# A decoder layer on one core: norm factors from replicated sums, router in column groups, reordered GLA opening, early modulation products

## The reference, cut to what matters

```python
mod = silu(c) @ ada_w + ada_b                  # six groups of 1024: sh1, sc1, gt1, sh2, sc2, gt2
h = rmsnorm(x, norm_mix_w) * (1 + sc1) + sh1
# h @ w_in is split; three branches: gated DeltaNet (o_a), GLA (o_b), Conformer convolution (o_c)
o_a = o / sqrt(mean(o*o) + eps) * dn_norm_w * silu(dn_z)
log_a = log_sigmoid(glr @ gla_gate_w + gla_gate_b) / 16
o_b = gla_recurrence(gq * 64**-0.5, gk, gv, log_a, S0)   # then its own gated RMSNorm
x = x + gt1 * (merged @ w_out)
u = rmsnorm(x, norm_ffn_w) * (1 + sc2) + sh2
s = sigmoid(u @ router_w)                      # 64 experts; top 8 of them, then the experts
x = x + gt2 * moe(u)
```

## Time and profile before

| | |
|---|---|
| median of 3 runs | 2899.44 us |
| profiled execution's own time | 2898.27 us |
| its span, first to last instruction | 2896.5 us |
| TensorE busy | 2755.3 us, 95% |
| VectorE, ScalarE, GpSimd busy | 37%, 20%, 28% |
| mean granted TensorE clock | 0.971 of full speed |

### The profile page before, as it was taken

How to read it: one execution, slowest core, us unless ns; L and a number is a source line. 1 busy time by engine, 2 the same in 40 slices (tenths; PEclk the granted TensorE clock), 3 DMA queues, 4 the chain that set the end, 5 groups by cost and what they waited for, 6 DMA issues and landing times. The chain is left out here.

```text
span 2896.5 us, 31387 instructions
## 1 busy us (share of the span) xinstructions
PE 2755.3 (95%) x10366; PEld 1626.5 (56%) x10367; DVE 1058.4 (37%) x1635; ACT 572.8 (20%) x1074; POOL 813.1 (28%) x992
## 2 busy tenths in 40 slices
PE   7997999997999899999999898999999999999996
PEld 4564888864666556666666566444444444444443
DVE  3333233334657677832111273322222222222224
ACT  3213333324434200011000230111111111111112
POOL 1000222101334000000000012555655555565553
PEclk8998999998999999999999898999999999999997
DMA  6520000021010111212112120688777788888874
GB/s 239 226 96 25 16 16 23 15 67 33 23 44 23 46 28 34 72 33 80 48 26 102 46 104 0 233 283 270 242 250 208 257 300 280 282 265 264 294 241 145
DMA packets 162802, 382.19 MB, mean 132 GB/s; under 512 B 24595, under 2 KB 111711, under 8 KB 134793
## 3 DMA queue, kind: packets, MB, share of 16 engines
q1 hardware_dynamic: 130449, 311.52, 30.2%
q0 software_dynamic: 32256, 69.33, 10.4%
HBM read 339.65 MB, written 72.94 MB: 142 GB/s over the span
## 5 line engine op out<-in xcount | busy, mean ns | idle before, releaser
L2568 PE MATMUL ps<-big 128*128 x1536 | 675.5, 593 | 3.2 <-SPq L2495 1.8
L2568 PEld LDWEIGHTS ps<-big 128*128 128x128 f32 x1536 | 284.3, 190 | 325.7 <-issue 325.7
L2520 POOL DMA_INDIRECT big<-u_rows,big x384 | 393.7, 1025 | 169.9 <-issue 85.4
L1756 PE MATMUL ps<-big 128*128 128x352 f32 x1152 | 346.8, 461 | 5.7 <-SPq L1692 5.7
L2578 PE MATMUL ps<-big 128*128 x768 | 345.8, 593 | 3.4 <-ACT big L2632 3.4
L1756 PEld LDWEIGHTS ps<-big 128*128 128x128 f32 x1152 | 219.7, 191 | 129.1 <-SPq L1692 6.1
L2673 DVE SCALAR_TENSOR_TENSOR big<-big,ps 128x256 f32<-128x256 f32 x96 | 64.0, 667 | 570.9 <-ACT big L2622 570.7
L2578 PEld LDWEIGHTS ps<-big 128*128 128x128 f32 x768 | 145.4, 190 | 188.4 <-issue 188.4
L846 PE MATMUL ps<-big 128*128 128x352 f32 x576 | 206.0, 464 | 2.1 <-DMA big<-in_w_in 2.0
L1301 PE MATMUL ps<-big 128*128 128x352 f32 x576 | 187.1, 473 | 12.8 <-DVE big L1521 7.8
L2536 POOL DMA_INDIRECT y_rows<-big x96 | 155.9, 1624 | 126.6 <-issue 61.2
(11 more groups left out here) (557 smaller groups left out, 3120.7 us busy)
## 6 DMA issues: line engine op xcount, KB each, us to landing
big<-in_exp_w_gate SPq DMA_DIRECT2D x64, 1024.0 KB
big<-in_exp_w_up SPq DMA_DIRECT2D x64, 1024.0 KB
big<-in_exp_w_down SPq DMA_DIRECT2D x64, 1024.0 KB
big<-in_ada_w SPq DMA_DIRECT2D x24, 1024.0 KB, 7.5
big<-in_w_in SPq DMA_DIRECT2D x48, 512.0 KB, 4.1
big<-in_w_in SPq DMA_DIRECT2D x6, 1024.0 KB, 5.3
big<-in_w_branch SPq DMA_DIRECT2D x24, 256.0 KB, 4.5
big<-u_rows,big POOLq DMA_INDIRECT x384, 5.9
```

The source lines that it names most:

```text
L1756: ins = pe.matmul(ps[:, c, 0:CW], ring_g[:, q % 2, j, :], k.hT[:, j, c * CW:(c + 1) * CW], start=(j == 0), stop=(j == KT - 1))
L2520: g.indirect_dma_start(out=x_rows[:, u, x * 256:(x + 1) * 256], out_offset=None, in_=u_quarters, in_offset=bass.IndirectOffsetOnAxis(idx_i ...
L2568: ins = pe.matmul(ps[:, 2 + u, :].rearrange("p (g f) -> p g f", f=FF), xT[:, u, j, :], gate_up[:, j], start=(j == 0), stop=(j == KT - 1))
```

## The change

Four places are edited.

1. `setup`: TensorE runs the first three modulation products ahead of its wait for the inverted norm factors, so ahead of their spread.
2. `gla_rule`: ScalarE takes the DeltaNet norm's root right after draining z 0, ahead of the units of gates 1. VectorE makes `keys(0, 0)` right after the reciprocal and `keys(0, 1)` after half of the spread. The four multiplications by `z` go from VectorE to GpSimd, behind its `queries` of chunk 2.
3. `project_out`: root and reciprocal are taken on all 128 partitions of the sum, so the turning, the small reciprocals and the spreading matmuls go. A root of a constant stands at ScalarE's start of the block.
4. `project_out`: the router's product runs in four quarters of 264 columns, whose results go to partitions 0 to 63 and 64 to 127 in turn; ScalarE copies two quarters of the logits out, VectorE the other two.

```diff
             # setup, TensorE
+            pe.wait_ge(c_copied, 1)
+            for x in range(3):
+                pe.wait_ge(ada_loaded[x], 16)
+                ada_product(k, pe, 6, slots[x], x).then_inc(ada_used, 1)
             pe.wait_ge(inverted, 1)
-            pe.wait_ge(c_copied, 1)
...
-            for x in range(KT):
+            for x in range(3, KT):
             # gla_rule, ScalarE
-            drain(ends[order["gates", 1, NCH - 1]])
+            drain(ends[order["z", 0, NCH - 1]])
             act.wait_ge(by_dve, drains("sum"))
             act.activation(fac[0:8, :], fac[0:8, :], ACT.Sqrt).then_inc(rooted, 1)
+            drain(ends[order["gates", 1, NCH - 1]])
             decays(0, 0)
             # gla_rule, GpSimd, after the queries of chunk i
+                if i == 2:
+                    g.wait_ge(by_act, drains("z", 3))
+                    for h in range(H):
+                        g.tensor_tensor(z[:, h, :], z[:, h, :], src[:, h, :], ALU.mult).then_inc(oa_done, 1)
             # gla_rule, VectorE
-                            v.wait_ge(by_dve, drains("spread", H - 1))
-                            v.wait_ge(by_act, drains("z", 3))
-                            for h in range(H):
-                                ins = v.tensor_tensor(z[:, h, :], z[:, h, :], src[:, h, :], ALU.mult)
-                            ins.then_inc(oa_done, 1)
-                            v.wait_ge(oa_done, 1)
+                            v.wait_ge(oa_done, H)
...
             v.reciprocal(fac[0:8, :], fac[0:8, :]).then_inc(inverted, 1)
+            keys(0, 0)
+            drain(ends[order["spread", 1, NCH - 1]])
+            keys(0, 1)
             drain(first_steps)
-            for p in range(2):
-                keys(0, p)
             # project_out, TensorE (the turn L2017 and the spread L2023 go)
+                for q in range(4):
+                    ins = pe.matmul(ps[E_N * (q % 2):E_N * (q % 2) + E_N, 3 + q // 2, 0:LW], rw[:, j, :], k.hT[:, j, q * LW:(q + 1) * LW],
+                                    start=(j == 0), stop=(j == KT - 1))
             # project_out, ScalarE
+            act.wait_ge(eps_ready, 1)
+            act.activation(warm[:, :], eps[:, :], ACT.Sqrt)
...
-            act.wait_ge(eps_ready, 1)
             act.wait_ge(summed, 1)
+            act.activation(root[:, 0:2 * CW].rearrange("p (c w) -> p c w", c=2), ps[:, 6:8, 0:CW], ACT.Sqrt, scale=1.0 / D, bias=eps[:, :])\
                .then_inc(rooted, 1)
+            act.activation(root[:, 2 * CW:T], ps[:, 0, 0:CW], ACT.Sqrt, scale=1.0 / D, bias=eps[:, :]).then_inc(rooted, 1)
...
+            for q in (0, 2):
+                act.activation(k.logits_T[:, q * LW:(q + 1) * LW], ps[0:E_N, 3 + q // 2, 0:LW], ACT.Copy).then_inc(stopped, 1)
             # project_out, VectorE
+            for r, cols in enumerate((slice(0, 2 * CW), slice(2 * CW, T))):
+                v.wait_ge(rooted, r + 1)
+                v.reciprocal(root[:, cols], root[:, cols]).then_inc(inverted, 1)
+            v.wait_ge(inverted, 2)
...
-                v.tensor_tensor(k.hT[:, j, 0:SEQ], k.xT[:, j, 0:SEQ], wide, ALU.mult).then_inc(normed, 1)
+                v.tensor_tensor(k.hT[:, j, 0:SEQ], k.xT[:, j, 0:SEQ], root[:, 0:SEQ], ALU.mult).then_inc(normed, 1)
...
+            v.wait_ge(logits, 1)
+            for q in (1, 3):
+                v.tensor_copy(k.logits_T[:, q * LW:(q + 1) * LW], ps[E_N:2 * E_N, 3 + q // 2, 0:LW]).then_inc(copied, 1)
```

More of the change, by code:

```diff
@@ L1958, in project_out @@
     sq, acc, root = w.take(2, T), w.take(T), w.take(T)
-    rw, rstd, eps = w.take(KT, E_N), w.take(NT), w.take(1)
+    rw, eps, warm = w.take(KT, E_N), w.take(1), w.take(1)
+    LW = T // 4
     filled, drained, added = k.sem("po_filled"), k.sem("po_drained"), k.sem("po_samples_added")
     router_loaded, shared_loaded, eps_ready = k.sem("po_router_loaded"), k.sem("po_shared_loaded"), k.sem("po_eps_ready")
-    squared, gathered, summed, rooted, turned, inverted, spread, normed, sampled, modulated, logits, dstep, stopped = (
-        k.sem("po_" + x) for x in ("squared", "squares_added", "summed", "rooted", "turned", "inverted", "spread", "normed", "sampled",
-                                   "modulated", "logits", "dve_step", "logits_copied"))
+    squared, gathered, summed, rooted, inverted, normed, sampled, modulated, logits, dstep, stopped, copied = (
+        k.sem("po_" + x) for x in ("squared", "squares_added", "summed", "rooted", "inverted", "normed", "sampled",
+                                   "modulated", "logits", "dve_step", "logits_copied", "logits_copied_by_vector"))
     zeroed, zeros_stored = k.sem("po_zeroed"), k.sem("po_zeros_stored")
@@ L2013, in _ @@
             ins.then_inc(summed, 1)
[L2014 to L2017, removed]
-            ins.then_inc(turned, 1)
-            pe.wait_ge(inverted, 2)
-            for t in range(NT):
-                n = tokens_of(t)
-                out = ps[:, 1 + t // 4, (t % 4) * P:(t % 4 + 1) * P] if t < 8 else ps[:, 7, 0:NS]
-                ins = pe.matmul(out, bcast(rstd[0:n, t:t + 1], P), k.ident[0:n, 0:n], start=True, stop=True)
-            ins.then_inc(spread, 1)
             pe.wait_ge(router_loaded, 32)
@@ L2029, in _ @@
                 pe.wait_ge(modulated, j + 1)
-                for c in range(NCH):
-                    ins = pe.matmul(ps[0:E_N, 3 + c, 0:CW], rw[:, j, :], k.hT[:, j, c * CW:(c + 1) * CW], start=(j == 0), stop=(j == KT - 1))
+                for q in range(4):
+                    ins = pe.matmul(ps[E_N * (q % 2):E_N * (q % 2) + E_N, 3 + q // 2, 0:LW], rw[:, j, :], k.hT[:, j, q * LW:(q + 1) * LW],
+                                    start=(j == 0), stop=(j == KT - 1))
             ins.then_inc(logits, 1)
@@ L2050, in _ @@
             act.wait_ge(logits, 1)
-            act.activation(chunks(k.logits_T), ps[0:E_N, 3:6, 0:CW], ACT.Copy).then_inc(stopped, 1)
+            for q in (0, 2):
+                act.activation(k.logits_T[:, q * LW:(q + 1) * LW], ps[0:E_N, 3 + q // 2, 0:LW], ACT.Copy).then_inc(stopped, 1)
         @block.vector
@@ L2066, in _ @@
                     v.tensor_tensor(acc[:, :], acc[:, :], sq[:, (m - 1) % 2, :], ALU.add).then_inc(gathered, 1)
-            v.wait_ge(turned, 1)
-            v.reciprocal(rstd[:, 0:8], ps[:, 6, 0:8]).then_inc(inverted, 1)
-            v.reciprocal(rstd[0:NS, 8:9], ps[0:NS, 6, 8:9]).then_inc(inverted, 1)
-            v.wait_ge(spread, 1)
+            for r, cols in enumerate((slice(0, 2 * CW), slice(2 * CW, T))):
+                v.wait_ge(rooted, r + 1)
+                v.reciprocal(root[:, cols], root[:, cols]).then_inc(inverted, 1)
+            v.wait_ge(inverted, 2)
             v.wait_ge(added, KT)
-            wide = ps[:, 1:3, :].rearrange("p a b -> p (a b)")
             scale = k.mod[:, 4 * KT:5 * KT, 1:NSEQ]
@@ L2075, in _ @@
             for j in range(KT):
-                v.tensor_tensor(k.hT[:, j, 0:SEQ], k.xT[:, j, 0:SEQ], wide, ALU.mult).then_inc(normed, 1)
+                v.tensor_tensor(k.hT[:, j, 0:SEQ], k.xT[:, j, 0:SEQ], root[:, 0:SEQ], ALU.mult).then_inc(normed, 1)
                 if j == 0:
-                    st(v.tensor_tensor(k.hT[:, :, SEQ:T], k.xT[:, :, SEQ:T], bcast(ps[:, 7, 0:NS].unsqueeze(1), KT, NS), ALU.mult))
+                    st(v.tensor_tensor(k.hT[:, :, SEQ:T], k.xT[:, :, SEQ:T], bcast(root[:, SEQ:T].unsqueeze(1), KT, NS), ALU.mult))
                     st(v.tensor_tensor(s, s, bcast(scale.unsqueeze(3), KT, SB, SL), ALU.mult))
                     v.tensor_tensor(s, s, bcast(k.mod[:, 3 * KT:4 * KT, 1:NSEQ].unsqueeze(3), KT, SB, SL), ALU.add).then_inc(sampled, 1)
+            v.wait_ge(logits, 1)
+            for q in (1, 3):
+                v.tensor_copy(k.logits_T[:, q * LW:(q + 1) * LW], ps[E_N:2 * E_N, 3 + q // 2, 0:LW]).then_inc(copied, 1)
 def plan_moe(k):
```

2 lines of the change are left out of this document (removed).

## The result

The changed kernel takes 2874.65 us (median of 4 runs, 2871.61 to 2881.24); the kernel before 2899.26 (4 runs, 2897.51 to 2901.99). The profiled execution took 2875.31, with a span of 2873.5: 23.0 less than before.

A forecast was written before the change was run, and what follows sets the result against it. TensorE was taken as busy nearly throughout, so gains must come from its stalls or removable work. Setup 1.5, GLA 6.1 and project_out 10.5 summed to 18.1, giving 2881.4, rounded to 2881; range 2876 to 2889.

The forecast's parts named there:

- a block that ends earlier moves all that follows by the same amount: Route and experts, behind the edits: nothing there waits for a fixed time, so gains pass through whole.
- slower, by the clock: Rival, chance 0.03: pauses between router tiles keep TensorE at 1.2 GHz through route, some 76 us longer, 2961 in all.
- Setup: Modulation products 0 to 2 ahead of the spread: pieces of ada_w decide; gain 1.5, bounds -2.9 and +2.4.
- the dry microseconds: Setup: DMA engines, 0.06 busy from 26 to 28, get used because pieces 4 to 6 are issued earlier.
- GLA's opening: Start of gla_rule: 5.4 from the wait for GpSimd's queries, 1.5 from full clock; together 6.9, bounds 4 and 7.5.
- The four multiplications: gla_rule, moved to GpSimd: the 4.76 saved are eaten by waiting for GpSimd's differences; -0.8, bounds +4.8 and -5.4.
- Project_out: Norm factors without turning or spread, router in column groups: gain 10.5; bounds 11.1 to a loss of 8.
- the long reciprocal: project_out: reciprocal over all 1056 columns takes 6.75 in two parts; first multiplication still comes 3.4 earlier.
- column groups side by side: project_out's router: passes on partitions 0 to 63 and 64 to 127 run two together, 0.92 per tile at full clock.
- the prediction's 0.23: project_out's router: estimated us for one pass of 264 columns at full clock, 0.46 at half.
- 205 us at half clock: Rival "slower, by the clock": time for place's 115.45 busy us if all ran at 0.50, some 76 us longer.
- four multiplications stretched by 2.98/2.1: Rival, chance 0.10: GpSimd multiplications slowed as queries beside keys were; -5.4 in place of -0.8, the whole 13.5, 2886.

The follow-up runs named there:

- e6: The kernel before with the last two of seven steps counting an expert's blocks of 128 tokens left out: median 2895.13 against 2899.49, ratio 0.9982.
- e5: The changed kernel with two VectorE writes of 128x64 ahead of place's first operands: place's three groups 5.49, 5.76 and 3.80 us; no median given.
- e11: The changed kernel with VectorE's first three spread steps put between the reciprocal and the first keys: median 2876.20, GLA 302.08 us.
- e16: The changed kernel with the four multiplications of 128x1056 back on VectorE: GLA 302.93 us, stall ahead of glu 5.97; no median given.
- e12: The changed kernel with keys behind the first spread steps and useless matmuls filling place's pauses and project_out's two pauses: median 2875.63, ratio 0.9914 of the kernel before.
- e10: The kernel before with 12, 20 and 12 useless matmuls in place's three pauses: median 2893.03 against 2900.49, ratio 0.9974.
- e8: The kernel before with 24, 40 and 24 useless matmuls in place's three pauses, outlasting them: median 2898.59, ratio 0.9998.
- e4: The kernel before with the project_out hunks alone: median 2886.50 against 2900.49, ratio 0.9945.

## Why the prediction was wrong

- **The step that failed** is "a block that ends earlier moves all that follows by the same amount". It looked for waits of fixed time in `route` and `experts` and found none; but the length of `route` depends on the clock behind three pauses of 3 to 5 us, and that depends on where they lie against the clock's changes. The second group began 65.54 to 65.58 us after the clock's last rise in four executions without the project_out part, and 65.39 to 65.46 after it in five with it and the pauses as they were: a difference of a tenth of a microsecond, worth 5.2 us. With e6 at 65.0 and e5 at 64.5, which are short too, the three groups were long only at the first place. `route` gave 7.2 so, where the forecast had 0; without them the time would have been inside the range. It could be seen ahead that something was loose there: the mean granted clock of that stretch was 0.89, and of groups of the same instructions three took 6.3 to 6.8 us and six 3.7 to 3.8. The sign could not be; what a shift the other way would have done no run shows. The rival "slower, by the clock" had the clock of `route` right as what could move the time, but set it off by pauses between the router's tiles, and knew only one sign.
- The Trainium skill's TensorE: Matmul & The Clock Gate, section What's actually happening, says that what the gate looks at runs on by itself and does not start anew with a kernel's work. The traces agree: after pauses equal to 0.01 us a group took 6.82 or 5.18.
- **Setup**: right in size (1.5 in the first pair of profiles, 2.6 in the second) and mechanism; the dry microseconds went (the DMA share from 26 to 28 is 1.01 instead of 0.06), and the first loads came earlier.
- **GLA's opening** was mis-sized: 6.9 forecast, 4.5 measured. Against the section's start the level matmuls began 2.94 earlier, where 5.4 was forecast, and they took 1.53 less by their clock, as forecast. The price of `keys(0, 0)` on VectorE was counted, 1.5, but not what an instruction with two SBUF operands behind a reciprocal of 6.7 us does to GpSimd; e11 gives 1.9 of it back. Up to the first `glu` step the section gained 4.8, at its end 3.7 are left: 1.0 went behind it, in part to the clock: one stretch at half clock there lasted 10.2 us instead of 6.8.
- **The four multiplications**: right in mechanism, and the -0.8 is not seen (e16: -0.3). ScalarE waits 4.53 for GpSimd's `differences` of chunk 3, and the stall ahead of `glu` stays.
- **Project_out**: right, 10.5 and 9.2 at like clock, column groups side by side and the long reciprocal included. That two column groups run side by side is shown best by e12's first tile: eight passes in 1.11 at full clock, where one after the other they would need 1.8 by the prediction's 0.23. In the profiled pair the sums found full clock as well, which the forecast did not have. They did so in all ten profiles with all three parts of the change (in three of these the pause ahead was filled), and in three of the eight without; why is not shown.
- Two figures of the rivals do not come out of their own terms, and the forecast does not hang on them: 205 us at half clock are 90 more than the 115 busy now, not 76; and four multiplications stretched by 2.98/2.1 give -5.0, not -5.4.
- `experts` was 2.0 longer in the profiled pair. With 17.8 from the parts, 7.2 from `route` and this, 23.0 come out.

## What to carry to other kernels

A pause on TensorE is not only lost time: behind the pauses of 3.3 and 5.0 us here, what followed ran at one of two clocks, and an edit far ahead changed for how long. Before forecasting an edit, look for equal groups of matmuls of unequal length behind such pauses, and put their spread into the range with both signs; to remove it, let TensorE work through the pause, with as much as the pause holds and no more (e10 gained 7.5 us, e8 nothing). Before placing a VectorE instruction with two SBUF operands behind a long one, see what GpSimd does in that time.

## What the hardware showed that was not expected

- `place`'s groups repeat to 0.02 us over executions whose `route` began anywhere from 1669.41 to 1674.63 on the span's clock. Against the clock's next rise all four began at the same place, 6.00 to 6.06 us ahead of it. e4's `route` began 6.32 ahead, 0.3 us earlier, and its second group came 65.42 instead of 65.54 to 65.58 after the rise: about half of the shift was left behind the stretch at half clock.
- GpSimd steps of 0.40 us stretch to 7.95 us, through a whole reciprocal that did not hinder them in the kernel before. The Trainium skill's SBUF — State Buffer, section SBUF: two separate sides, names an exclusive lock between a GpSimd instruction that reads SBUF and a VectorE one with two SBUF operands. The trace agrees, and goes further: GpSimd already stood still while the VectorE instruction with two SBUF operands was only next in the queue, 6.5 us before it began. e11 shows that the order decides; how the queue does it no run shows.
- Two VectorE writes of together 0.3 us (e5) changed which of VectorE and GpSimd came first and moved `place` by 0.9 us the other way.
